# Cross attention's output projection in another order: by column halves for both token tiles, the first tile's transposes behind it

## What is computed

```python
for layer in range(DEPTH_2):                    # 2 layers
    ...                                         # mixer, first normalisation
    xa = mem_cross_attention(h, mem, xa_wq[layer], xa_wkv[layer], xa_wo[layer])   # ends in o @ wo, 1024 x 1024
    h = layer_norm_2(DN_ALPHA * h + xa, ln2_g[layer], ln2_b[layer])
    ff = hier_moe(h, ...)                       # router: h @ (1024 x 36); top 2 of 8 experts in the best of 4 groups
    h = layer_norm_2(DN_ALPHA * h + ff, ln3_g[layer], ln3_b[layer])
```

## Time and profile before

| | us |
|---|---|
| median of 3 runs (2834.72 to 2838.29) | 2835.69 |
| the profiled execution, its time | 2830.84 |
| the profiled execution, its span | 2829.1 |
| PE busy | 2520.5 (89%) |
| DVE busy | 1226.6 (43%) |
| ACT busy | 381.3 (13%) |

### The profile page before, as it was taken

The page is one execution under the profiler, slowest core; times in us unless marked ns, Lnnn a source line. Parts: engine busy times, 40 slices in busy tenths (PEclk is TensorE's granted clock), DMA queues, the critical chain, the costliest instruction groups (busy, mean ns, idle before and its releaser), DMA issues.

```text
span 2829.1 us, 37953 instructions
## 1 busy us (share of the span) xinstructions
PE 2520.5 (89%) x16098; PEld 1634.7 (58%) x16098; DVE 1226.6 (43%) x2543; ACT 381.3 (13%) x865; POOL 210.5 (7%) x224
## 2 busy tenths in 40 slices
PE   9999999999999999999999999866658999766665
PEld 5779755796568957699457785322223675322221
DVE  4766645676456757786646642000002453000002
ACT  1410002100031001310022111000000412000000
POOL 0300013000120000400003000000000310000000
PEclk9999999999999999999999999988888999987888
DMA  8354544544526436265341868999999547999998
GB/s 322 120 163 158 187 135 129 184 160 163 181 96 194 157 126 206 89 194 179 121 150 30 313 246 323 422 420 422 421 421 383 202 185 301 421 421 421 421 421 341
DMA packets 245773, 703.57 MB, mean 249 GB/s; under 512 B 18795, under 2 KB 123753, under 8 KB 197219
## 3 DMA queue, kind: packets, MB, share of 16 engines
q1 hardware_dynamic: 244304, 699.30, 65.4%
q10 hardware_dynamic: 1299, 1.83, 0.2%
HBM read 698.20 MB, written 1.05 MB: 247 GB/s over the span
## 4 chain that ended last, share of the span: by engine, by line
PE 73%; DMA 21%; SPq 2%; ACT 2%; DVE 2%; issue 1%; DVEq 0%; ACTq 0%
PE lin L916 45%; PE sco L916 16%; PE trp L916 9%; DMA ring<-in_moe_w_down 6%; DMA ring<-in_moe_w_gate 3%; DMA ring<-in_moe_w_up 3%; DMA arena<-in_moe_w_gate 3%; DMA arena<-in_moe_w_down 3%; DMA arena<-in_moe_w_up 2%; SPq L748 2%; PE trp L1085 1%; PE trp L1181 1%; ACT arena L2327 0%; ACT arena L2303 0%; DMA x<-in_moe_w_down 0%
## 5 line engine op out<-in xcount | busy, mean ns | idle before, releaser
L916 PE MATMUL lin<-ring,arena 128*128 128x512 f32 (+4 forms) x1852 | 679.7, 517 | 2.6 <-ACT arena L2303 1.3
L916 PE MATMUL sco<-arena 128*32 128x512 f32 (+6 forms) x2528 | 548.3, 514 | 112.8 <-DMA ring<-in_moe_w_up 26.1
L916 PEld LDWEIGHTS lin<-ring,arena 128*128 128x128 f32 (+1 forms) x1852 | 344.2, 190 | 292.0 <-issue 268.5
L916 PE MATMUL sco<-ring,arena 128*32 128x512 f32 (+2 forms) x1620 | 393.8, 711 | 131.8 <-DMA arena<-in_moe_w_up 39.6
L916 PEld LDWEIGHTS sco<-arena 128*32 128x32 f32 (+3 forms) x2528 | 195.9, 149 | 284.1 <-issue 274.0
L916 PE MATMUL lin<-arena 128*128 128x128 f32 (+8 forms) x2824 | 339.5, 297 | 3.5 <-ACT arena L2303 1.3
L3714 DVE TENSOR_TENSOR arena<-arena,sco 128x512 f32<-128x512 f32 x16 | 11.0, 687 | 759.4 <-PE sco L916 759.4
L916 PEld LDWEIGHTS lin<-arena 128*128 128x128 f32 (+3 forms) x2824 | 262.2, 169 | 61.1 <-issue 42.2
L916 PEld LDWEIGHTS sco<-ring,arena 128*32 128x32 f32 (+1 forms) x1620 | 102.5, 134 | 277.0 <-issue 268.9
L916 PE MATMUL trp<-arena 128*128 128x128 f32 (+2 forms) x1584 | 217.6, 292 | 0.9 <-ACT arena L2490 0.7
L916 PE MATMUL lin<-arena,ring 128*128 128x128 f32 (+1 forms) x1720 | 207.3, 284 | 0.7 <-DVE arena L3643 0.7
(11 more groups left out here) (364 smaller groups left out, 2335.5 us busy)
## 6 DMA issues: line engine op xcount, KB each, us to landing
ring<-in_w_gate_up SPq DMA_DIRECT2D x88, 1024.0 KB, 5.9
ring<-in_moe_w_up SPq DMA_DIRECT2D x66, 1024.0 KB, 26.7
ring<-in_moe_w_down SPq DMA_DIRECT2D x65, 1024.0 KB, 27.0
ring<-in_moe_w_gate SPq DMA_DIRECT2D x61, 1024.0 KB, 26.7
arena<-in_moe_w_gate SPq DMA_DIRECT2D x54, 1024.0 KB, 26.8
arena<-in_moe_w_up SPq DMA_DIRECT2D x51, 1024.0 KB, 26.4
arena<-in_moe_w_down SPq DMA_DIRECT2D x47, 1024.0 KB, 26.7
ring<-in_w_down SPq DMA_DIRECT2D x44, 1024.0 KB, 5.4
```

The costliest lines, as they stand in the source:

```text
L916: return nc.tensor.matmul(o, lhsT, rhs, start=start, stop=stop, skip_group_check=not one_group)
```

## The change

The loops of the output projection are turned: column half outside, tile inside. So the order is left half of tile 0, left half of tile 1, right half of tile 0, right half of tile 1. DVE is told of tile 0 after the right half of tile 0. The transposes of tile 0 leave the projection and stand in `moe`, behind four products of filler (two in layer 1) and ahead of the router's products of tile 0, which wait for all evacuations. The filler behind the router's products of tile 0 is 6 in place of 8 products (3 in place of 4 in layer 1), and the one between the small products is 4 in place of 6 (1 in place of 2).

```diff
@@ output_linear
-                for t in range(NT):
-                    done = 0
-                    for c in range(2):
+                for c in range(2):
+                    for t in range(NT):
                         for b in range(KD):
                             if t == 0 and b % 4 == 0:
                                 w.append(ring[:, slot(), :].rearrange("p (k n) -> p k n", k=4))
-                            if t == NT - 1 and done == 10:
-                                x_columns(0)
...
                             last = mm(lin[:, 2 * t + c, :], srcT[:, b, t * P:(t + 1) * P], w[2 * c + b // 4][:, b % 4, :],
                                       start=b == 0, stop=b == KD - 1)
-                            done += 1
                             if t == NT - 1 and b % 4 == 3:
                                 last.then_inc(slots_used, 1)
-                    if t == 0:
-                        last.then_inc(pe_for_vec, 1)
+                        if t == 0 and c == 1:
+                            last.then_inc(pe_for_vec, 1)
@@ moe
-                await_transposes()
                 s = slot(5)
...
+                pe.wait_ge(y_taken, t_taken.n - 1)
+                values(4 if values_ahead(layer) else 2)
+                x_columns(0)
+                await_transposes()
                 w = ring[:, s, 0:KD * 36].rearrange("p (k n) -> p k n", k=KD)
                 for t in range(NT):
                     if t == 1:
-                        values(8 if values_ahead(layer) else 4)
+                        values(6 if values_ahead(layer) else 3)
                         x_columns(1, 1)
                         await_transposes(1)
...
-                values(6 if values_ahead(layer) else 2)
+                values(4 if values_ahead(layer) else 1)
```

## The result

The changed kernel took 2838.24 us in the median of 20 runs (2834.28 to 2844.2), the kernel before 2834.88 us in 20 runs beside them (2830.35 to 2838.69). The ratio is 1.0015, with a 95% interval of 1.0008 to 1.0021: slower by about 4 us, and inside the 0.2% that the prediction took for "what this kernel's measurement can't tell from no change"; with 20 runs of each kernel it can, since the interval lies above 1. The span of the profiled execution is 2833.8 us in place of 2829.1.

What follows compares the result with a forecast made beforehand. Expert stages were taken as DMA-bound, their continuous stream starting when PE and DVE finish routing. A delay of 1.88 us in each layer, +3.8 on the median 2835.69, gave 2839.4 us; range 2834 to 2843.

Steps and rivals of the forecast that it cites:

- 35.69 us: Layer 0, projection's start to tile 1's transposes: 35.69 us after the change instead of 33.81, so 1.88 us later.
- Two fewer there let PE wait 0.9 us for DVE and save nothing.: Later filler, layer 0, 4 products in place of 6: PE waits 0.9 us for DVE, with no time saved.
- DVE: Routing, layer 0: whole-tile addition 6.8 us later, DVE's chain 0.4 us shorter, but PE reaches tile 1's transposes later still.
- All loads from 1721.79 on shift by 1.88 us ... so the continuous stream starts 1.88 us later.: SP queue, layer 0: routing's delay moves these loads and the start of continuous DMA by 1.88 us, same bytes to come.
- From there on there is no gap.: Kernel before, layer 0: once the loads of 1735.84 arrive at 1737.3, the DMA stream runs without a gap.
- Worth of the earlier pair: 0.: Two projection-slot loads per layer, issued 6.8 us earlier, gain 0; bounds 0 and −2 × 2.49 us per layer.
- the rival's 10 us: Rival: the earlier loads let the stream start with less to move, −10 us in two layers, 2829.5 us; chance 0.04.
- The shift is hidden.: Rival: DMAs still have work when shifted loads come; one layer hidden 2837.6, both 2835.7; 0.20 together with a DVE-bound case.
- TensorE's clock falls.: Rival: new waits thin PE's work in the routing and lower its clock, +7.7 us per layer, 2855; chance 0.03.
- +3.8 us: Whole kernel: routing shifts of both layers summed, put on the median 2835.69, giving 2839.4 us.

Runs made afterwards that it cites:

- experiment 3: Kernel before, plus six products nobody reads ahead of the filler before tile 1's transposes, both layers: 2843.81 us against 2834.42, ratio 1.0031.
- experiment 4: Kernel before, plus the same six unread products in the fourth round of experts, inside the DMA stream: 2834.31 us against 2834.42, ratio 1.0003.
- experiment 6: Kernel before, with SP alone holding loads into the last ring slots until the first expert products free a slot: 2849.74 us against 2833.44, ratio 1.0057.
- experiment 2: Changed kernel, with two filler products (one in layer 1) between tile 0's transposes and router products: 2834.46 us against 2834.42 before, ratio 0.9998.
- experiment 5: Changed kernel, with the left half's two slots reported free at later products, so their loads go out late: 2838.71 us against 2833.0 before, ratio 1.0018.
- Experiment 7: Changed kernel, wait filled, six products ahead of tile 1's transposes (three in layer 1), layer 0's last two behind the gather: ratio to before 1.0002, another chip 1.0004.
- experiment 8: Kernel before, with layer 0's last two filler products moved behind the gather: 2833.82 us against 2834.02, ratio 1.0001.
- experiment 1: Changed kernel with the filler counts of before, none ahead of tile 0's transposes: 2836.19 us against 2834.42 before, ratio 1.0005.
- The changed kernel's second profile: The changed kernel unaltered, run again beside the late-loads kernel on the same chip: 2840.39 us (6 runs), ratio to before 1.0028.

## Why the prediction was right, point by point

- **"35.69 us" to tile 1's transposes.** Measured 35.67 in layer 0 and 35.65 in layer 1. The terms: projection 27.46 (forecast 27.47), head filler 1.73 (1.77), transposes with both evacuations 1.77 (1.76), router products 2.03 (2.04), filler 2.68 (2.65). PE's wait for ACT is 0.74 us where I wrote "0.9", although the distance from transposes to products, which I had built from the evacuations' row, is right. The bracket counts from the end of the transposes' row, 1.04 us long, and I had counted from its distance to the next start, 0.87.
- **"Two fewer there let PE wait 0.9 us for DVE and save nothing."** It waits 0.68 us in layer 0 and 1.55 in layer 1 (forecast 0.9 and 1.6). The gather shifts by 1.85 us, so nothing was saved. That it is 0.2 smaller than forecast in layer 0 is the same difference: the filler's eight records ahead of it stand as 1.95 us, and their starts are worth 1.77. In layer 1 I had added to a bracket, 0.69, and no difference is left.
- **DVE.** Whole-tile addition 6.86 us later (forecast 6.8); tile 1 normalised 32.71 us after the projection's start, 0.57 earlier than before (forecast 0.4). As forecast, PE doesn't need it by then.
- **"All loads from 1721.79 on shift by 1.88 us ... so the continuous stream starts 1.88 us later."** The issues of 1735.84 shift by 1.86 us. That a shift there comes out at the end is shown from both sides: delayed on PE ahead of the stream it does (experiment 3: 10.3 us put in, 9 out), delayed by the same products within it it doesn't (experiment 4), and delayed at SP alone with PE as it was it does again (experiment 6: 16.5 us in the trace, 16 in the time). One sentence ahead of it was too smooth: "From there on there is no gap." In the kernel before the windows 8 and 9 us behind the gather of layer 0 show 285 and 360 GB/s, so the stream has a dip there. The dip is the same in the changed kernel (295 and 373) and costs it nothing more, but it is where the kernels of experiments 2 and 5 move fewer bytes than before.
- **"Worth of the earlier pair: 0."** Shown by experiments 2 and 5: with the pair early and the routing as before the time is that of before, and the changed kernel without the early pair is not slower than with it. The window from 1706 to 1712 us, 4 GB/s, shows the engines running empty again behind the pair. The times can't see a worth under some 3 us; the rival's 10 us they exclude.
- **"The shift is hidden."** Refuted for delays of 5 us and more by experiments 3 and 6. For the 1.85 us of the change itself only the cut of the profile says it (3.71 us in the two stretches, no later stretch shorter); the two medians of the changed kernel, +3.4 and +7.4 us, show that it isn't zero and size it only loosely. If a part of the +7.4 is the change's own, no run here shows which.
- **"TensorE's clock falls."** The granted clock in the routing of the changed kernel is 1.00 in both layers. The lower level does appear in the routing of five other profiles, two of them with the order of before, and with PE fully busy while it lasts; the last section shows one of them. It isn't what this change costs.
- **The total.** "+3.8 us", 2839.4, against 2838.24 measured and +3.4 us between the medians (about +4.3 by the ratio). Most of the forecast's distance from the median is the base: 2835.69 in the first three runs of before, 2834.88 in the twenty. That the time fell into the range, 2834 to 2843, says little, because the range took in the hidden case too. What bears the prediction out is the terms in the trace and experiments 2, 3 and 6.

The cause of the slowdown is thus not the order that gives the change its name. It is that the transposes of tile 0, once hidden within the projection, came to stand in front of a wait with nothing behind them (0.9 us, and 0.1 for the router products behind it), and that two more filler products were put ahead of tile 1's transposes (0.9 us), in each of two layers.

**Experiment 7, where I was wrong.** "Tile 1 early" should have given 1.6 us. The step that failed is that an earlier gather is an earlier stream. In layer 0 the gather's gain of 0.7 us was paid with a hole in the loads, which experiment 8 shows alone. In layer 1 the 0.7 us stays, and the sum is close to nothing, as the time says.

What the hole costs is less sure than that it is there. Experiment 8's first stage is 1.7 us longer than before, but so are those of two kernels that leave the last filler where it was: 456.60 us with the wait filled and 456.33 with the loads as late. These stages go with fewer bytes in their opening. The first twelve microseconds behind the gather, in the kernel before, the wait-filled one and that of experiment 8:

```profile
1729.48:1741.48 12.00, 10.63 (x93) 5.57 (x96) 1.34 (x8) 2.48 (x3) 0.00 (x0) 1.00 0.99 373
1729.91:1741.91 12.00, 10.63 (x93) 5.56 (x96) 1.34 (x8) 2.48 (x3) 0.00 (x0) 1.00 0.93 338
1730.59:1742.59 12.00, 11.31 (x96) 6.17 (x100) 1.34 (x8) 2.48 (x3) 0.00 (x0) 1.00 0.88 335
```

It holds for all twelve profiles: six with 369 to 376 GB/s in these twelve microseconds have stages of 454.5 to 455.3 us, five with 305 to 354 have 456.3 to 457.0, and experiment 6, with 141, has 461.56. In experiments 7 and 8 a part of the loss is the hole. In the wait-filled kernel it comes 8 to 10 us behind the gather, 225 and 190 GB/s where the kernel before has 285 and 360, and its PE's and SP's rows up to there are those of before. What held those loads wasn't tried and stays open.

## What to carry to other kernels

When a long stage is bound by loads, ask only when its stream of loads becomes continuous, and follow each edit to that moment: in this kernel what PE did ahead of it counted nearly in full (9 of 10.3 us), and what it did in the one place tried behind it counted nothing. A load that went out early into an empty stretch was worth nothing that the runs could see; the rows put that down to the next slot, which was freed by the same event as before, though no run here frees it sooner. Filler has two effects besides its length, the wait that it covers and the buffer that its last product frees; moving it for the one can cost the other. If transposes are moved out of a dense block, move filler behind them in the same edit, since their evacuation is a wait of its own.

## What the runs showed of the hardware that I had not expected

The granted clock fell to its lower level, 1.2 GHz, for a few microseconds while PE had no gap at all. In the routing shown here PE had waited 0.25 us for ACT at 1724.20, as every kernel here does at this step, and was busy from then on. Windows of the tile-1-early kernel in its first run, layer 0, and the filler that runs in them:

```profile
1726.00:1727.00 1.00, 1.00 (x10) 0.97 (x10) 0.49 (x4) 0.93 (x4) 0.00 (x0) 1.00 0.97 410
1727.00:1728.00 1.00, 1.00 (x4) 0.82 (x3) 0.86 (x7) 0.00 (x0) 0.00 (x0) 0.53 0.91 279
1728.00:1729.00 1.00, 1.00 (x3) 0.76 (x3) 0.89 (x6) 0.48 (x3) 0.00 (x0) 0.50 0.87 369
1729.00:1730.00 1.00, 1.00 (x4) 0.79 (x3) 0.84 (x7) 0.00 (x0) 0.00 (x0) 0.50 1.08 451
```

```profile
1726.71 4.50 PE L916 MATMUL lin<-ring,spare 128*128 128x256 f32 x12
```

Twelve records take 4.50 us where the same twelve take 2.81 in other profiles: 1.7 us lost. The same kernel on another chip had none there, but one in layer 1. It also struck the routing of the kernels of experiments 1, 3 and 4, the last in both layers; the last two have the order of before.

The stretch from the first stage to the next projection shows the same thing. It takes 160.14 to 160.16 us in six profiles and 161.82 to 161.84 in five; in each of the five, and in none of the six, the granted clock is under 1.00 for some four microseconds of it, with PE fully busy. One window of the wait-filled kernel, and the same of the changed one:

```profile
2203.00:2211.00 8.00, 8.00 (x39) 7.04 (x39) 7.19 (x12) 0.22 (x1) 5.53 (x6) 0.79 1.03 402
2203.00:2211.00 8.00, 8.00 (x49) 7.33 (x49) 7.15 (x9) 0.23 (x2) 5.12 (x5) 1.00 1.02 407
```

The changed kernel's second profile, with 164.75 us, has 0.57 from 2204 to 2212 and a second spell later. So it comes in some executions and not in others, whatever the order of the work, and one spell is of the size of one layer's share of this change. The Trainium skill (TensorE: Matmul & The Clock Gate, "Why this matters for your kernels") ties the lower level to idle gaps; the four windows from 1726 to 1730 us, with PE busy for 1.00 of each 1.00 us while the clock falls, don't agree. What sets it off isn't known from these runs.
